# Gathering four expert rows of 32 tokens at a time, with weighted sums in four column quarters of TensorE

## The chip, the cores and the metric

The kernel runs on one core of one Trainium2 chip. The metric is the device time of one execution in microseconds, the lower the better; the median of several runs is compared. The traces come from one profiled execution of each kernel.

## What is computed

A decoder trunk of two layers over 256 tokens of width 1024, all in float32. Layer 0 mixes tokens with an S5 state-space layer (a complex diagonal scan over the positions, GELU, a gated projection); layer 1 with dilated sliding-window attention in three groups of 16 heads. Each layer ends in PEER, a channel mixer that fetches single-neuron experts. For each token and each of 8 heads it scores two halves of product keys, takes the best 16 of each, and of their sums the best 16: 128 experts for each token, with softmax gates. Then, for h the normalised token:

```python
def chunk_fn(args):
    hc, ic, gc = args
    act = jnp.einsum('cd,ckd->ck', hc, u_tab[ic])
    return jnp.einsum('ck,ckd->cd', gc * jax.nn.gelu(act), v_tab[ic])
```

The row of U and the row of V of an expert lie side by side, 2048 floats, 8 KB. A token fetches 128 of them, and the whole kernel 256 tokens x 128 x 2 layers: 537 MB of the 685 MB that it moves.

## The kernel before

The tokens are two chunks of 128, one token to a partition. There are four phases of gather: layer 0 with chunk 0 and 1, layer 1 with chunk 0 and 1. In each phase 128 gathers bring, each, one expert row for each of the 128 tokens (1.05 MB). They go two by two (a pair, 64 of them in a phase) through a ring of eight slots:

- POOL adds the two parts of the row numbers (L788), reads one of them back (L792) and issues two indirect DMAs (L794), after TensorE and VectorE are done with the pair four pairs back (L785, L786).
- VectorE takes the dot product of the U half of each slot with H (L826), ScalarE the gelu of two dots (L635), VectorE multiplies by the gates (L830).
- ScalarE builds a diagonal matrix of the weights (L639), and TensorE multiplies it with the V half of the slot, two matmuls of 512 columns that add up in PSUM banks 0 and 1 (L393). An f32 matmul shows as two weight loads and two MATMUL instructions in the trace.
- Where `both_on_pe` holds (the first 44, 8, 8 and 0 pairs of the four phases) both rows of a pair go to TensorE. Elsewhere the second is summed by VectorE (L838), and otherwise VectorE only sets a flag (L834).

The order on every engine is written out by hand. Class `Gather` has a method `at(phase, n)`, which puts the pairs up to n of a phase into an engine's stream; the rest of the work stands between such calls. So the second chunk's S5 (L929 to L972 on VectorE, L448 to L472 on TensorE, from pair 14 on, four pairs to each of eight steps) runs under phase 0. Layer 1 of chunk 0 runs under phase 1, of chunk 1 under phase 2: norm, three quarters of the top-k in twelve parts, 18 projections (L412) with a 2 MB weight load each, heads (L527 to L563, L1113), output projection, norm, key projections (L422). Phase 3 has only the top-k parts under it, three pairs apart, and the last norm of chunk 0. The top-k of a quarter of the heads is in four parts (L1015 to L1086); its row numbers are known when `idx_ready` rises (L1085), for which POOL waits once in a quarter (L801). Weights go by SyncE's queue into two buffers in turn (L343), each load when TensorE has used the buffer.

The norm (L852 to L862) squares on VectorE, takes the root on ScalarE (L645) and writes H, of which there is one for each chunk. At the end of a phase VectorE adds the banks to X (L850).

S5 on VectorE has eight tiles in two sets (M) for its products; the outputs come from matmuls with 32 columns of weights (L469), in an order that finishes one 32-partition strip of the bank before the next. Its inputs come from matmuls with 32 rows (L455).

```python
def pair(phase, b, r, first):
    ...
    if not first:
        pool.wait_ge(v_pe, b * SETS + (phase * PAIRS_G + r - SETS + 1))
        pool.wait_ge(v_dve, b * SETS + (phase * PAIRS_G + r - SETS + 1))
```

## Time and profile before

| | |
|---|---|
| runs | 1946.47, 1946.58, 1944.43 us; median 1946.47 |
| profiled execution | 1946.0 us, span 1944.2 |
| busy PE, DVE, ACT, POOL | 1388.8 (71%), 1444.4 (74%), 421.5 (22%), 874.3 us (45%) |
| mean granted TensorE clock | 0.873 |
| DMA | 685.04 MB (read from HBM 683.01), mean 352 GB/s |
| queue of the gathers | 536.90 MB, 69.4% of the 16 engines' span |
| queue of the weights | 147.20 MB, 18.3% |
| chain that ended last | PE 32%, DVE 30%, DMA 25%, issue 5%, ACT 4%, POOL 3% |

PE is TensorE's matmuls, PEld its weight loads, DVE is VectorE, ACT is ScalarE, SP is SyncE. The span goes from the first to the last instruction; the execution's own time is 1.8 us longer. The time of the phases can be read from the dot products: their first ones start at 187.9, 634.3, 1126.9 and 1593.3 us, and the last at 1930.8. A clock of 1.00 is 2.4 GHz, 0.50 is 1.2 GHz; a figure between is the mean of a stretch with both.

### The profile page before, as it was taken

How to read it: one execution, taken by the hardware profiler on the slowest of the kernel's cores; microseconds unless marked ns; L12 is line 12 of the kernel's file. 1: busy time of each engine (PE TensorE's matmuls, PEld its weight loads, DVE VectorE, ACT ScalarE, POOL GpSimd, SP SyncE). 2: the span in 40 equal slices, each digit the busy share in tenths (PEclk: the TensorE clock that was granted, in tenths of full speed). 3: DMA queues.
4: the chain of work that ended last, by engine and by line, in shares of the span. 5: the costliest groups of instructions: out<-in, count | busy, mean ns of one | idle time of the engine just before them, and what ended most of it. 6: DMA issues, size and time to landing. Idle time of an engine off the chain costs nothing.

```text
span 1944.2 us, 16899 instructions
## 1 busy us (share of the span) xinstructions
PE 1388.8 (71%) x4848; PEld 713.1 (37%) x4848; DVE 1444.4 (74%) x3260; ACT 421.5 (22%) x911; POOL 874.3 (45%) x1031
## 2 busy tenths in 40 slices
PE   1676766777976698898777559979987765544554
PEld 1446223333454243543536124355454541111111
DVE  8944987777568887655657788776576699899776
ACT  4011211111121212402411121162163111111111
POOL 0002443344444334344343853355465557666763
PEclk9888888889988899799789779999999887787777
DMA  7017977888999899899699989999999999999997
GB/s 287 1 66 288 348 282 298 318 330 322 369 423 422 317 404 424 310 421 423 254 408 411 412 342 390 425 403 380 425 406 375 422 353 389 378 366 365 414 421 300
DMA packets 88638, 685.04 MB, mean 352 GB/s; under 512 B 12144, under 2 KB 12272, under 8 KB 14320
## 3 DMA queue, kind: packets, MB, share of 16 engines
q0 software_dynamic: 73728, 536.90, 69.4%
q1 hardware_dynamic: 14832, 147.20, 18.3%
q8 instruction: 37, 0.61, 0.1%
q14 instruction: 41, 0.34, 0.0%
HBM read 683.01 MB, written 1.05 MB: 352 GB/s over the span
## 4 chain that ended last, share of the span: by engine, by line
PE 32%; DVE 30%; DMA 25%; issue 5%; ACT 4%; POOL 3%; POOLq 0%; SPq 0%; DVEq 0%
DMA ringmem<-experts,rows_now 16%; PE ps L393 12%; DVE ringmem L826 10%; PE ps L412 10%; DMA wt<-w_qkv 6%; PE ps L422 4%; DVE X L838 2%; DVE area L954 2%; DMA wt<-w_o 2%; PE ps L469 2%; POOL ringmem L794 2%; PE ps L536 2%; ACT gelus L635 1%; PE ps L561 1%; ACT diag L639 1%
## 5 line engine op out<-in xcount | busy, mean ns | idle before, releaser
L393 PE MATMUL ps<-ringmem,diag 128*128 128x512 f32 x1264 | 743.7, 729 | 416.5 <-ACT diag L639 416.0
L826 DVE CUSTOM_DVE_ANT_0 ringmem<-ringmem,H 128x1024 f32<-128x1024 f32 x512 | 610.8, 1220 | 86.0 <-DMA ringmem<-experts,rows_now 83.8
L794 POOL DMA_INDIRECT ringmem<-experts,rows_now x512 | 602.1, 1176 | 130.6 <-issue 118.3
L393 PEld LDWEIGHTS ps<-ringmem,diag 128*128 128x128 f32 x1264 | 265.0, 226 | 819.8 <-ACT diag L639 563.9
L788 POOL TENSOR_TENSOR rows_now<-row_a,row_b 128x2 uint32 (+1 forms) x256 | 130.5, 510 | 895.2 <-PE ps L393 708.3
L635 ACT ACTIVATE gelus<-dots 128x2 f32<-128x2 f32 x256 | 52.2, 204 | 993.6 <-DVE dots L826 993.3
L412 PE MATMUL ps<-wt,hT 128*128 128x512 f32 x576 | 254.5, 595 | 15.1 <-DMA wt<-w_qkv 15.1
L838 DVE SCALAR_TENSOR_TENSOR X<-ringmem,wts,X 128x1024 f32<-128x1024 f32 x196 | 251.9, 1285 | 7.5 <-DVE wts L830 0.5
L412 PEld LDWEIGHTS ps<-wt,hT 128*128 128x128 f32 x576 | 107.9, 190 | 158.1 <-issue 154.5
L792 POOL TENSOR_TENSOR tick<-rows_now 128x1 uint32<-128x1 uint32 x256 | 137.0, 535 | 20.2 <-POOL rows_now L788 0.3
L639 ACT ACTIVATE diag<-con,wts 128x128 f32<-128x128 f32 x316 | 120.3, 398 | 61.3 <-DVE wts L830 61.3
L830 DVE TENSOR_TENSOR wts<-gelus,gate 128x2 f32<-128x2 f32 x256 | 41.2, 161 | 111.6 <-ACT gelus L635 111.6
L422 PE MATMUL ps<-hT,wt 128*128 128x128 f32 x1024 | 119.9, 279 | 5.0 <-DMA wt<-w_q 3.8
L422 PEld LDWEIGHTS ps<-hT,wt 128*128 128x128 f32 x1024 | 118.8, 195 | 12.3 <-DMA wt<-w_q 6.3
L1104 DVE TENSOR_TENSOR area<-ps,con 128x512 f32<-128x512 f32 x24 | 16.6, 692 | 74.4 <-PE ps L412 74.3
L469 PE MATMUL ps<-area 128*32 128x128 f32 x512 | 51.0, 333 | 29.2 <-DVE area L972 29.2
L412 PE MATMUL ps<-wt,gT 128*128 128x512 f32 x128 | 62.0, 642 | 9.8 <-DMA wt<-w_o 8.4
L635 ACT ACT_TABLE_LOAD x50 | 64.2, 1283 | 0.9
L469 PEld LDWEIGHTS ps<-area 128*32 128x32 f32 x512 | 42.8, 134 | 37.0 <-DVE area L972 31.5
L1119 DVE CUSTOM_DVE_ANT_0 area<-ps,area 128x384 f32<-128x384 f32 (+1 forms) x32 | 24.2, 755 | 43.1 <-PE ps L536 43.1
L1019 DVE MAX8 qs<-ps 128x8 f32<-128x128 f32 x64 | 14.2, 283 | 43.8 <-PE ps L443 43.8
L954 DVE TENSOR_TENSOR_SCAN area<-area 128x128 f32<-128x128 f32 x128 | 45.8, 431 | 0.1
(155 smaller groups left out, 1132.4 us busy)
## 6 DMA issues: line engine op xcount, KB each, us to landing
wt<-w_qkv SPq DMA_DIRECT2D x36, 2048.0 KB, 11.5
wt<-w_q SPq DMA_DIRECT2D x16, 2048.0 KB, 11.8
wt<-w_glu SPq DMA_DIRECT2D x5, 2048.0 KB, 8.1
ringmem<-experts,rows_now POOLq DMA_INDIRECT x512, 10.1
wt<-w_o SPq DMA_DIRECT2D x4, 2048.0 KB, 14.8
ringmem<-w_glu SPq DMA_DIRECT2D x3, 2048.0 KB, 16.9
gain<-gains SPq DMA_DIRECT2D x9, 512.0 KB, 9.2
area<-keys SPq DMA_DIRECT2D x4, 1024.0 KB, 9.8
```

What stands on the lines that cost most here:

```text
L393: last = pe.matmul(ps[:, n, :], diag[:, r, i, :], ring[:, 2 * r + i, D + n * 512:D + (n + 1) * 512], start=(first and i == 0), stop=final, ...
L412: last = pe.matmul(ps[:, bank, :], act[:, k, :], wt[:, n % 2, k, :], start=(k == 0), stop=(k == KT - 1))
L422: last = pe.matmul(ps[:, bank, m * P:(m + 1) * P], wt[:, n % 2, k, m * P:(m + 1) * P], hT[:, k, :], start=(k == 0 and m == 0), stop=(k == ...
L469: last = pe.matmul(ps[32 * q:32 * (q + 1), 2, 0:P], CW[:, PPT * k + q, w, :], m[:, q, :], start=(i == 0), stop=(i == 3))
L635: act.activation(gelus[:, 2 * r:2 * r + 2], dots[:, 2 * r:2 * r + 2], ACT.Gelu_apprx_tanh).then_inc(gelu_ready, 1)
L639: last = act.activation(diag[:, r, i, :], ident, ACT.Copy, scale=wts[:, 2 * r + i:2 * r + i + 1])
L788: pool.tensor_tensor(rows_now[:, r, :], row_a[:, c, at], row_b[:, c, at], ALU.add).then_inc(rows_ready, 1)
L792: pool.tensor_tensor(tick[:, :], rows_now[:, r, 0:1], rows_now[:, r, 0:1], ALU.add)
L794: pool.indirect_dma_start(ring[:, 2 * r + i, :], None, experts[phase // NC], bass.IndirectOffsetOnAxis(ap=rows_now[:, r, i:i + 1], axis=0) ...
L826: last = v.tensor_tensor_reduce(ring[:, i, 0:D], ring[:, i, 0:D], H[:, c, :], 1.0, 0.0, ALU.mult, ALU.add, dots[:, i:i + 1])
L838: v.scalar_tensor_tensor(out=X[:, c, :], in0=ring[:, 2 * r + 1, D:2 * D], scalar=wts[:, 2 * r + 1:2 * r + 2], in1=X[:, c, :], op0=ALU.mult ...
L954: last = v.tensor_tensor_scan(dst[:, q, :], mag[:, n:n + 1].to_broadcast([P, P]), src[:, q, :], z0[:, n:n + 1] if c else 0.0, ALU.mult, AL ...
```

## The change

A gather now takes four expert rows of each of 32 tokens. Four gathers (a quad, 32 of them in a phase) serve all 128 tokens, and the bytes are the same. In slot j of a quad the partitions hold tokens 32j to 32j+31 four times over, each time with another expert. What follows from it:

- H is needed in four spread copies: Hrep[:, j] holds the 32 rows of quarter j four times. TensorE makes them with a matrix of repeated identities (`spread_h`), eight matmuls of 32 rows and 512 columns in each phase, and ScalarE copies each out of PSUM, at the start of a phase. There is one H instead of two, and the norm that writes it next waits for these matmuls.
- The weights are a matrix S[:, b, j] of 128 x 32 for each slot: the small identity times gate times gelu, two VectorE products for a quad. The diagonals on ScalarE, the flags and VectorE's own sums are gone.
- TensorE multiplies S[:, b, j], 32 columns, with the V half of the slot into partitions 32j to 32j+31 of banks 0 and 1: eight matmuls in a quad, the four j in turn for each half.
- The gelu is taken of four dots at once, and a slot is free again when its whole quad has gone through TensorE.
- The top-k gives floats of row number and gate for a quarter (`sel`). ScalarE lays them out anew with 16 copies of 32 partitions, and makes the row numbers integers with one more, before `idx_ready` rises. POOL's adds and reads are gone, and its instructions and all loops are written out.
- S5 has seven tiles instead of eight, with more ordered steps; its weights have two parts instead of three, with the sign put into a product; its matmuls are ordered so that the strips alternate. Keys, projected queries and head tiles share a smaller area, with the waits that this needs; the counts of PSUM use in attention are split in two semaphores.

```diff
-        H = sb("H", [P, NC, D])
+        H = sb("H", [P, D])
+        Hrep = sb("Hrep", [P, QUAD, D])
...
             def at(self, phase, n):
...
+                end = STEPS * phase + 2 * min(n, PAIRS_G)
+                while self.done < end:
+                    self.slot(self.done)
                     self.done += 1
...
         def _(pe):
+            def slot(s):
+                q, j = divmod(s, QUAD)
+                if j < QUAD - 1:
+                    return
+                phase, n = divmod(q, QUADS)
+                pe.wait_ge(s_ready, q + 1)
+                if n == 0 and phase:
                     pe.wait_ge(peer_done, phase)
...
+                for half in range(2):
+                    for j in range(QUAD):
+                        last = pe.matmul(ps[TG * j:TG * (j + 1), half, :], S[:, q % 2, j, :],
+                                         ring[:, (QUAD * q + j) % RING,
+                                              D + half * 512:D + (half + 1) * 512],
+                                         start=(n == 0), stop=(n == QUADS - 1), skip_group_check=True)
                 last.then_inc(v_pe, 1)
...
+            def spread_h(phase):
+                pe.wait_ge(normed, norm_event(phase // NC, phase % NC, 1) + 1)
+                for j in range(QUAD):
+                    rows_j = slice(TG * j, TG * (j + 1))
+                    for half in range(2):
+                        n = 2 * QUAD * phase + 2 * j + half
+                        if j:
+                            pe.wait_ge(hrep_ready, n - 1)
+                        pe.matmul(ps[:, 2 + half, :], rep[rows_j, :], H[rows_j, half * 512:(half + 1) * 512],
+                                  start=True, stop=True, skip_group_check=True).then_inc(h_spread, 1)
...
             layer0(None, 0)
+            spread_h(0)
             layer0(0, 1)
             g.at(0, PAIRS_G)
+            spread_h(1)
             layer1(1, 0)
             g.at(1, PAIRS_G)
+            spread_h(2)
             layer1(2, 1)
             g.at(2, PAIRS_G)
+            spread_h(3)
...
         def _(act):
+            def spread_h(phase):
+                if phase:
+                    act.wait_ge(dots_ready, QUADS * phase)
+                for j in range(QUAD):
+                    for half in range(2):
+                        act.wait_ge(h_spread, 2 * QUAD * phase + 2 * j + half + 1)
+                        act.copy(Hrep[:, j, half * 512:(half + 1) * 512],
+                                 ps[:, 2 + half, :]).then_inc(hrep_ready, 1)
...
             def gate_quarter(ph, i):
                 act.wait_ge(best_ready, QUARTERS * ph + i + 1)
+                act.activation(gex, gex, ACT.Exp).then_inc(gate_exp, 1)
+                n = QPQ * i
+                act.wait_ge(sel_ready, QUARTERS * ph + i + 1)
+                for j in range(QUAD):
+                    for r in range(QUAD):
+                        last = act.copy(lay[TG * r:TG * (r + 1), ph % NC, :, j, n:n + QPQ],
+                                        sel[TG * j:TG * (j + 1), :, QPQ * r:QPQ * (r + 1)])
+                link(last)
+                act.copy(rows[:, ph % NC, :, n:n + QPQ],
+                         lay[:, ph % NC, 0, :, n:n + QPQ]).then_inc(idx_ready, 1)
...
         def _(pool):
+            for s in range(2 * NC * STEPS):
+                phase, at = divmod(s, STEPS)
+                n, j = divmod(at, QUAD)
+                if at % QSTEPS == 0:
+                    pool.wait_ge(idx_ready, QUARTERS * phase + at // QSTEPS + 1)
+                if s >= RING:
+                    pool.wait_ge(v_pe, (s - RING) // QUAD + 1)
+                pool.indirect_dma_start(
+                    ring[:, s % RING, :], None, experts[phase // NC],
+                    bass.IndirectOffsetOnAxis(ap=rows[:, phase % NC, j, n:n + 1], axis=0)
+                ).then_inc(landed[s % RING], 16)
...
         def _(v):
+            def slot(s):
+                q, j = divmod(s, QUAD)
+                phase, n = divmod(q, QUADS)
+                c, b, i = phase % NC, q % 2, s % RING
+                if n == 0:
+                    v.wait_ge(hrep_ready, 2 * QUAD * phase + 2 * j + 2)
+                v.wait_ge(landed[i], 16 * (s // RING + 1))
+                last = v.tensor_tensor_reduce(ring[:, i, 0:D], ring[:, i, 0:D], Hrep[:, j, :],
+                                              1.0, 0.0, ALU.mult, ALU.add, dots[:, b, j:j + 1])
+                if j < QUAD - 1:
+                    return
                 last.then_inc(dots_ready, 1)
...
+                if q >= 2:
+                    v.wait_ge(v_pe, q - 1)
+                shape = [P, QUAD, TG]
+                link(v.tensor_tensor(S[:, b], spread(own, 1, shape), spread(lay[:, c, 1, :, n], 2, shape),
+                                     ALU.mult))
+                v.wait_ge(gelu_ready, q + 1)
+                v.tensor_tensor(S[:, b], S[:, b], spread(gelus[:, b, :], 2, shape),
+                                ALU.mult).then_inc(s_ready, 1)
...
-            def norm(gphase, start, c, e, done, count):
+            def norm(gphase, start, c, e, done, h_free, count):
...
+                if count:
+                    v.wait_ge(h_free, count)
+                v.scalar_tensor_tensor(out=H[:, :], in0=X[:, c, :], scalar=stat[:, 3:4],
...
             def s5_rotate(c, k):
...
+                v.tensor_tensor(T1, co, bre, ALU.mult)
+                v.tensor_tensor(T2, si, bim, ALU.mult)
+                link(v.tensor_tensor(T3, si, bre, ALU.mult))
+                link(v.tensor_tensor(T1, T1, T2, ALU.add))
+                v.tensor_tensor(T2, co, bim, ALU.mult).then_inc(bu_used, 1)
                 v.wait_ge(bu_used, u + 1)
+                link(v.tensor_tensor(T2, T2, T3, ALU.subtract))
```

## Rows read from the trace of the kernel before

**Rows 1.** Busy time by stretch: us, engines busy (instructions), PE clock, DMA share, GB/s.

```profile
180.00:274.00 94.00, 56.26 (x104) 22.54 (x104) 79.22 (x271) 21.44 (x47) 43.85 (x58) 0.82 0.89 340
274.00:487.00 213.00, 154.39 (x602) 72.90 (x602) 161.76 (x347) 30.88 (x103) 88.64 (x128) 0.87 0.83 311
487.00:634.00 147.00, 114.99 (x480) 66.24 (x478) 98.24 (x194) 24.76 (x55) 65.32 (x83) 0.88 0.98 405
634.00:1127.00 493.00, 388.97 (x1208) 199.82 (x1208) 339.39 (x764) 116.73 (x248) 220.84 (x255) 0.88 0.94 379
1127.00:1593.00 466.00, 390.39 (x1448) 214.55 (x1448) 342.90 (x757) 140.85 (x259) 233.25 (x253) 0.94 0.96 391
1593.00:1804.00 211.00, 102.66 (x152) 33.63 (x152) 192.62 (x432) 31.37 (x85) 138.49 (x153) 0.78 0.95 375
1804.00:1931.00 127.00, 71.42 (x100) 22.04 (x100) 97.21 (x153) 17.89 (x53) 77.26 (x93) 0.78 1.00 415
...
778.00:826.00 48.00, 38.64 (x142) 24.66 (x143) 29.49 (x61) 22.37 (x44) 16.90 (x25) 0.79 0.80 309
826.00:923.00 97.00, 86.84 (x219) 38.30 (x218) 54.88 (x96) 16.61 (x38) 42.03 (x45) 0.96 1.01 422
923.00:972.00 49.00, 38.45 (x143) 25.29 (x142) 29.85 (x61) 20.99 (x41) 16.48 (x26) 0.74 0.69 255
```

**Rows 2.** The chain of waits under S5 of the second chunk: start, us, what.

```profile
277.65 10.01 PE ps L393 x16
```

**Rows 3.** Groups by line: operation, count, busy us, mean ns, idle before them, its releaser.

```profile
L393 PE MATMUL ps<-ringmem,diag 128*128 128x512 f32 x1264 | 743.7, 729 | 416.5 <-ACT diag L639 416.0
...
L838 DVE SCALAR_TENSOR_TENSOR X<-ringmem,wts,X 128x1024 f32<-128x1024 f32 x196 | 251.9, 1285 | 7.5 <-DVE wts L830 0.5
...
L830 DVE TENSOR_TENSOR wts<-gelus,gate 128x2 f32<-128x2 f32 x256 | 41.2, 161 | 111.6 <-ACT gelus L635 111.6
```

**Rows 4.** Groups by line, small VectorE and ScalarE operations.

```profile
L739 ACT COPY area<-ps 128x512 f32<-128x512 f32 x24 | 14.1, 589 | 55.0 <-PE ps L523 55.0
...
L1110 DVE TENSOR_TENSOR area<-area 128x256 f32<-128x256 f32 x24 | 10.2, 425 | 0.8
...
L670 ACT ACTIVATE gate<-gate 128x32 f32<-128x32 f32 x16 | 3.7, 230 | 0.2
```

**Rows 5.** The timeline of two pairs in the last stretch: start, us, engine, operation.

```profile
1820.19 1.22 DVE L826 CUSTOM_DVE_ANT_0 ringmem<-ringmem,H 128x1024 f32<-128x1024 f32 x1
...
1821.45 0.20 ACT L635 ACTIVATE gelus<-dots 128x2 f32<-128x2 f32 x1 [4.60 <-DVE dots L826]
...
1822.34 3.27 PE L393 MATMUL ps<-ringmem,diag 128*128 128x512 f32 x4 [3.45 <-ACT diag L639]
...
1825.80 1.02 POOL L788 TENSOR_TENSOR rows_now<-row_a,row_b 128x2 uint32 x1 [1.82 <-PE ps L393]
...
1827.24 0.97 POOL L794 DMA_INDIRECT ringmem<-experts,rows_now  x1 [0.15 <-issue]
...
1827.69 1.98 PE L393 MATMUL ps<-ringmem,diag 128*128 128x512 f32 x4 [2.09 <-ACT diag L639]
...
1828.51 1.96 POOL L794 DMA_INDIRECT ringmem<-experts,rows_now  x1 [0.30 <-issue]
```

**Rows 6.** Busy time of L469 alone, 66 to 68 us: PE, PEld, clock, DMA.

```profile
66.00:68.00 2.00, 2.00 (x20) 1.70 (x20) 0.50 0.00 0
```

**Rows 7.** The timeline of TensorE at 72 us.

```profile
71.89 0.75 PE L455 MATMUL ps<-hT,area 32*128 32x128 f32 x16
```

**Rows 8.** Line 794 alone, from issue to landing.

```profile
DMA to landing us min/median/max: 5.3/10.1/27.6
```

**Rows 9.** The timeline at the end of the first phase.

```profile
627.46 1.23 DVE L826 CUSTOM_DVE_ANT_0 ringmem<-ringmem,H 128x1024 f32<-128x1024 f32 x1 [0.61 <-DMA ringmem<-experts,rows_now]
...
637.80 1.28 ACT L647 ACT_TABLE_LOAD   x1
...
639.53 1.29 DVE L861 SCALAR_TENSOR_TENSOR H<-X,stat,gain 128x1024 f32<-128x1024 f32 x1
```

More of the change, by code:

```diff
@@ L268, in build, with __init__ @@
         class Gather:
-            def __init__(self, eng, pair):
-                self.eng, self.pair, self.done = eng, pair, 0
+            def __init__(self, slot):
+                self.slot, self.done = slot, 0
             def at(self, phase, n):
@@ L451, in s5_bu @@
                     pe.wait_ge(bu_used, u)
-                for q in range(PPT):
-                    rows = slice(32 * q, 32 * (q + 1))
-                    for r in range(2):
-                        last = pe.matmul(ps[:, 4 + q, r * P:(r + 1) * P], WB[rows, k, r, :],
-                                         hT[rows, k, :], start=True, stop=True, skip_group_check=True)
+                for r in range(2):
+                    for q in range(PPT):
+                        quad = slice(32 * q, 32 * (q + 1))
+                        last = pe.matmul(ps[:, 4 + q, r * P:(r + 1) * P], WB[quad, k, r, :],
+                                         hT[quad, k, :], start=True, stop=True, skip_group_check=True)
                 last.then_inc(bu_ready, 1)
@@ L819, in link @@
                 v.wait_ge(dve, steps[0])
-            def pair(r, b, phase, bp, first, final, both):
-                c = phase % NC
-                for i in (2 * r, 2 * r + 1):
-                    v.wait_ge(landed[i], b * 16 + 16)
-                    last = v.tensor_tensor_reduce(ring[:, i, 0:D], ring[:, i, 0:D], H[:, c, :],
-                                                  1.0, 0.0, ALU.mult, ALU.add, dots[:, i:i + 1])
-                last.then_inc(dots_ready, 1)
-                v.wait_ge(gelu_ready, b * SETS + (r + 1))
-                v.tensor_tensor(wts[:, 2 * r:2 * r + 2], gelus[:, 2 * r:2 * r + 2],
-                                gate[:, c, bass.ds(bp * RING + 2 * r, 2)], ALU.mult).then_inc(wts_ready, 1)
-                v.wait_ge(wts_ready, b * SETS + (r + 1))
-                if both:
-                    v.tensor_copy(passed[:, :], wts[:, 2 * r:2 * r + 1]).then_inc(v_dve, 1)
-                    return
-                if not (first and phase == 0):
-                    v.wait_ge(v_dve, b * SETS + r)
-                v.scalar_tensor_tensor(out=X[:, c, :], in0=ring[:, 2 * r + 1, D:2 * D],
-                                       scalar=wts[:, 2 * r + 1:2 * r + 2], in1=X[:, c, :],
-                                       op0=ALU.mult, op1=ALU.add).then_inc(v_dve, 1)
@@ L844, in peer_end @@
+            g = Gather(slot)
             def peer_end(phase):
```

282 lines of the change are left out of this document (115 added, 167 removed).

## The prediction

> **What bounds the kernel now.** I read first the busy time by stretch, cut where the dot products change their pace. The DMA share is near 1, and the rate 422 GB/s, in the stretch from 826 to 923 us [rows 1]: that is the fastest rate held for long. Against it each stretch has room of its length times (1 - rate/422): 18 us in 180 to 274, 56 in 274 to 487, 6 to 634, 49 to 1127, 34 to 1593, 24 to 1804, 2 to 1931 [rows 1]: 189 us. The bytes don't change, so no schedule of them gains more: 1946 - 189 = 1757 us is the floor. The two stretches of attention heads of the first chunk, 778 to 826 and 923 to 972, ran at 309 and 255 GB/s [rows 1]: 13 + 19 of the 49.
>
> Who holds back the DMA differs. In 274 to 487 (S5 of the second chunk over the first gather) the chain of waits goes through 10 us of weighted-sum matmuls, one after another, ahead of the next S5 input [rows 2], while VectorE is busy 162 of 213 us [rows 1]. In 1593 to 1804 (the last gather over the top-k) VectorE is busy 193 of 211 [rows 1]. In 1804 to 1931 the DMA binds, at 415 GB/s. Groups by line give the sizes: 744 us of TensorE in L393, 252 of VectorE in the sums at L838 [rows 3].
>
> **What goes and comes.** Per four rows (a quad): out go two weight products, eight diagonal builds at most, 16 matmul instructions of full width (or half of them, with two sums on VectorE at 1.285 us [rows 3]), and two adds and two ticks on POOL. In come two VectorE products of 128x128 and 16 matmul instructions of 32 columns. VectorE's products: 128x256 takes 0.425 [rows 4], 128x2 0.161 [rows 3]; between them I take 0.3 each, and keep both as bounds (256 of them at the upper end would be 33 us more over the run, half of it under the DMA).
>
> TensorE, the disputed price. A pair of these instructions (one f32 matmul of 512 columns) takes about 0.86 us at full clock, 2.4 GHz (1.98 for four with the tail), and 1.7 at the half, 1.2 GHz (3.27 for four, partly at each) [rows 5]. Do four column quarters run at once? In the S5 outputs, also 32 columns wide, 20 instructions of 128 columns started in 2.00 us at a granted clock of 0.50 [rows 6]; one such instruction alone lasts about 0.21 us at that clock (a quarter of 0.85), so two quarters ran at once, there in an order that serves one quarter eight times in a row. Row strips in the S5 inputs did 16 in 0.75 us [rows 7], where one by one at full clock is 1.7: all four at once. The change alternates quarters, as these. So a quad costs from 2 x 0.86 + 0.2 = 1.9 us (four at once, full clock) to 8 x 1.7 = 13.7 (none at once, half clock). I take four at once, 1.9 full, 3.7 half, as rows 7 is nearest in order. The Trainium skill (TensorE: Matmul & The Clock Gate, Part 3) gives 3.07 times for four row strips and 2.38 for three column strips, not the ideal; by it a quad is 13.7/3.07 = 4.5 us at half clock, and the sum below would be some 20 us worse, in the last gather mostly; no row here shows four column strips.
>
> **The ring.** It was freed by pairs, four of them; now by quads, two. Gathers at the full rate land 2.47 us apart (1.05 MB at 422 GB/s). The shortest issue to landing is 5.3 us [rows 8]. A slot's successor must land five spacings, 12.3 us, after the quad's last landing, so its issue may come 7.0 us after it. The chain: dot and gelu 1.46 (1820.19 to 1821.65), product 0.4, matmuls 3.7, POOL 0.2 (1825.61 to 1825.80), with half a microsecond of waits [rows 5]: 6.2. That fits by 0.8 us, by 2.6 at full clock. POOL loses the 1.4 us of add and tick (1825.80 to 1827.24); but its issue lasted 1.96 instead of 0.97 when a dot ran beside it [rows 5], which can eat the rest. Before, the same slot had three more pairs, 14.8 us, as cover.
>
> **The sum**, against the profiled execution (1946.0 us, span 1944.2; median of the runs 1946.47).
> - S5 under the gather, 8 steps of 26.6 us (POOL's 128 instructions, four a pair, make 32 pairs). VectorE is busy 20.2 per step [rows 1]; it loses 4 x 0.16 (weights) and as many flags, gains 4 x 0.3, has some 0.3 for three more ordered waits, and waits some 2 us in all for gelus: 22.5. TensorE's 10 us become under 4, off the path; S5's products wait for the outputs before them, done a step earlier. (22.5 - 26.6) x 8 = -33.
> - Top-k ahead of it, 180 to 274, and at the first quads of the second gather: VectorE-bound (79 of 94 us busy [rows 1]), no L838 there, so the same work: -3 with the rest up to 634.
> - Heads, first chunk: 11 pairs, TensorE's share of a pair falls from 3.4 to 1.85 at half clock, and ScalarE switches its table for gelu half as often: -1.7 each, -18. Second chunk: -9, within its room there. Projection stretches are at the DMA's rate already; other transitions -5. TensorE's projections have less company; each is 16 instructions of 0.43, 6.9 us at full clock; at 0.85, between the 0.96 and 0.74 of rows 1, it is 8, and its 2.1 MB with its pair's take the DMA 9.9: covered by 1.9.
> - Last gather, 1593 to 1804: 153 POOL instructions make 38 pairs of 5.55 us [rows 1]. Of that 2.4 are dots, 0.46 weights with their wait, 1.285 the sum, so 1.4 the third of a top-k part (4.2 us). Now 2.4 + 0.5 + 1.4 = 4.3, under the 4.93 of the DMA. Parts that fall inside a quad delay its end by some 1.5 us, of which 0.8 is covered, nine times with the rest: I recover 13 of the 24 us.
> - New, the four copies of H at each phase: eight matmuls and eight ScalarE copies of 0.589 us [rows 4], alternating over two banks, behind the last quad's matmuls and ahead of the square root of the next norm on ScalarE. From the last dot's start: quad done 5.7, matmuls to 15, copies to 15.8, table switch (1.28 [rows 9]) and root to 17.3, norm done 18.9; now it is done 13.4 after (627.46 to 640.82) [rows 9]. +5.5 at two boundaries; at the third the DMA runs dry: the fourth copy at 16.4, quad freed 22.5, data 25.3, against 19.7 when the other quad has landed: +5.6. Together +17. Below zero is excluded, as the copies wait for the last dots; above, 14 us of matmuls at half clock make it 30.
> - New, 17 small ScalarE copies per quarter, 0.230 us for the nearest row [rows 4], 4 us: later quarters lie 2 or more pairs ahead of need and are covered by those pairs' transfers; without that cover each costs 4. ScalarE waits there for VectorE's selection, with the next quad's gelu queued behind; VectorE does no dot meanwhile, so that gelu isn't asked for. The first is on the path, and the second chunk's norm now waits for the copies of H: +5.
> - POOL's other adds and ticks: nothing, since POOL waited for TensorE; it is the ring's 1.4 us, counted. SyncE's order and bytes stay. The loops written out: nothing, as most steps were written out before and no row shows a wait for instructions; if POOL's 512 issues did wait for them, it would be B.
> Sum: -33 - 3 - 27 - 5 - 13 + 17 + 5 = -59: **1887 us**, on the profiled time.
>
> **Rivals.**
> A. Nearly all the room is used: jitter hides in VectorE's freed time, boundaries hide behind landed quads. Two thirds of 189: 1820 us. For: 59 + 22 of cost is only 81. Against: VectorE-bound stretches keep their work. 0.12.
> B. Slower, the shallow ring. Place: every quad where gathers alone feed the DMA. Point: last landing to next issue over 7.0 us. At 9 (half clock, POOL held by a dot, a ScalarE or TensorE block in between) the 32 quads of the last gather lose 2 each, 64, the 13 go, and ten quads elsewhere lose 20: 1887 + 97 = 1984. For: 6.2 against 7.0, and TensorE gets less to do, with the granted clock already 0.78 in both last stretches [rows 1]. Against: S5 stretches leave 22.5 per 19.8. 0.14.
> C. The quarters don't run at once, so the change doesn't do what it says. Then a quad takes 6.9 us at full clock, the chain 9.3, the last gather loses 32 x 2.3 = 74, and S5 and heads gain nothing: 1946 + 74 + 22 - 13 = 2029. Against: rows 6. 0.05.
> D. The boundaries and inner pauses give the gains back, by the 30 us bound and double losses in quads: 1930 to 1950. 0.09.
> Another floor: were the DMA held to its mean of 352 GB/s, nothing would be gained; rows 1 hold 422 over 97 us. The Trainium skill (DMA: Bandwidth & Descriptors, Bandwidth) speaks of about 358 GB/s per core with both cores of a pair streaming, and of 425 for one alone; by the first, 683 MB take 1908 us and D would be likeliest; the trace goes with the second.
>
> **Numbers.** The forecast has 0.60 (own range 1850 to 1930, from the bounds of the quad price, the boundaries and heads). About 0.2% (4 us) is what can be told from no change. Faster: 0.60 + 0.12 + 0.04 of D = 0.76; same 0.05; slower 0.14 + 0.05 = 0.19. 1845 to 1975 leaves out two thirds of A, C and half of B: 0.2.
>
> **What would show it.** Four weighted-sum matmuls with starts a few ns apart, a quad in 1.9 or 3.7 us; VectorE near 1444 - 252 - 50 + 77 = 1219 us; S5 steps of 22.5 us; the rate in 1593 to 1804's counterpart over 395 GB/s; dots idle about 9 us at each phase start. Wrong, if the pure gather at the end runs under 400 GB/s (B), or quads take 7 us or more (C).

## The result, and the profile after

The changed kernel takes **1978.15 us** (median of four runs, 1969.89 to 1980.83), against 1946.35 for the kernel before on the same chip (1944.43 to 1946.58): a ratio of 1.0158, interval 1.0126 to 1.0191. It is 32 us slower, where 1887 and "faster" were forecast; 1978 lies 3 us above the range of 1845 to 1975. The profiled execution has a span of 1979.0 us and a mean granted TensorE clock of 0.729, where it was 0.873. It is the slowest of the four runs, so tables that are read from it can be some microseconds too long beside a median.

The page of the changed kernel: busy time and share by engine, clock in tenths over 40 slices, DMA, the chain that ended last, and the groups that the change brings (operation, count, busy us, mean ns, idle time ahead of them and its releaser).

```profile
PE 1131.4 (57%) x5696; PEld 545.9 (28%) x5696; DVE 1220.7 (62%) x2986; ACT 319.6 (16%) x748; POOL 542.8 (27%) x519
PEclk9878556667785897896886579879867876555555
DMA packets 88642, 685.21 MB, mean 346 GB/s; under 512 B 12144, under 2 KB 12272, under 8 KB 14320
DMA 34%; PE 32%; DVE 20%; POOL 6%; issue 5%; ACT 2%; SPq 0%; POOLq 0%; DVEq 0%; ACTq 0%
...
L816 POOL DMA_INDIRECT ringmem<-experts,lay x512 | 539.0, 1053 | 1412.2 <-PE ps L380 1115.0
L839 DVE CUSTOM_DVE_ANT_0 ringmem<-ringmem,Hrep 128x1024 f32<-128x1024 f32 x512 | 617.0, 1224 | 367.8 <-DMA ringmem<-experts,lay 357.3
L380 PE MATMUL ps<-ringmem,S 128*32 128x512 f32 x2048 | 390.9, 904 | 653.1 <-DVE S L852 653.1
L852 DVE TENSOR_TENSOR S<-S,gelus 128x128 f32<-128x128 f32 x128 | 37.5, 293 | 48.1 <-ACT gelus L644 34.3
L690 ACT COPY lay<-sel 32x16 f32<-32x16 f32 x256 | 51.5, 201 | 66.8 <-DVE sel L1096 64.0
L397 PE MATMUL ps<-H,con 32*128 32x512 f32 x64 | 45.6, 1017 | 3.3 <-ACT Hrep L656 3.3
```

All engines have less to do, as intended: TensorE 1131 us instead of 1389, VectorE 1221 (the forecast said 1219) instead of 1444, POOL 543 instead of 874. Yet the run is longer. Two lines point to where to look. POOL now stands idle for 1115 us until a weighted-sum matmul (L380) frees ring slots; before, it waited 708 us for L393. And the clock row (PEclk) ends in six fives, half clock, 1.2 GHz. Neither shows by itself that time is lost.

Busy time by stretch, the counterparts of [rows 1] (from and to, us, then PE, PEld, DVE, ACT and POOL busy with instructions, PE clock, DMA share, GB/s). First top-k, S5, the rest of the first gather, the second and third gathers, the last gather over the top-k, the pure gather at the end; below, gathers 320 to 347, with projections and then the second half of the second chunk's heads.

```profile
187.00:275.00 88.00, 28.30 (x111) 6.63 (x110) 78.15 (x258) 21.33 (x56) 24.45 (x27) 0.53 0.86 328
275.00:460.00 185.00, 56.48 (x592) 19.94 (x592) 161.56 (x312) 10.18 (x41) 68.37 (x63) 0.66 0.89 355
460.00:614.00 154.00, 103.23 (x574) 56.04 (x575) 77.44 (x179) 19.16 (x44) 44.91 (x43) 0.78 0.98 404
614.00:1119.00 505.00, 344.59 (x1448) 170.60 (x1448) 273.40 (x690) 89.15 (x211) 131.27 (x128) 0.76 0.91 369
1119.00:1625.00 506.00, 375.05 (x1691) 201.49 (x1690) 278.59 (x693) 107.16 (x218) 141.12 (x131) 0.80 0.90 362
1625.00:1835.00 210.00, 74.07 (x315) 13.37 (x313) 151.23 (x394) 26.11 (x85) 79.00 (x77) 0.58 0.96 383
1835.00:1966.00 131.00, 43.36 (x192) 7.14 (x192) 66.61 (x123) 5.23 (x15) 46.11 (x45) 0.55 0.96 387
...
1379.00:1490.00 111.00, 86.39 (x380) 51.30 (x380) 49.45 (x103) 26.82 (x41) 31.28 (x28) 0.76 0.89 357
```

And the same gathers (320 to 347 of 512) in the kernel before:

```profile
1377.00:1470.00 93.00, 81.21 (x327) 46.73 (x325) 65.07 (x117) 41.55 (x69) 54.67 (x55) 0.96 0.99 403
```

S5 gained what it should (213 us at 311 GB/s became 185 at 355). The third gather, at 391 GB/s before, fell to 362; the clock of gathers 320 to 347 from 0.96 to 0.76. The last stretch fell from 415 GB/s to 387 though DMA is all it has to do; under 400 was the forecast's own sign for rival B.

A table in stages that don't depend on where a window is cut: microseconds between the first dot products of the named gathers (gather 0 to 511; a phase has 128). Q, K and V are the projections ahead of the heads, WO is the one behind them.

```
stage, gathers           before   after  change
to the first dot          187.9   195.4   +7.5
0-24 (top-k)               86.2    79.6   -6.6
24-88 (S5)                211.3   185.2  -26.1
88-128                    148.9   153.7   +4.8
128-184 (QKV, heads)      234.0   241.1   +7.1
184-256 (QKV, heads, WO)  258.7   264.5   +5.8
256-296 (QKV)             157.2   161.0   +3.8
296-320 (heads, QKV)       92.5    98.8   +6.3
320-348 (QKV, heads)       93.1   110.8  +17.7
348-384 (heads, WO)       123.6   134.8  +11.2
384-456 (top-k)           199.7   192.6   -7.1
456 to the end            151.2   161.7  +10.5
```

The heads themselves fill shorter stretches, two in each chunk (us, with the granted clock):

```
gathers          before        after
163-174          45.0 (0.77)   46.5 (0.59)
196-208          48.6 (0.72)   41.7 (0.63)
292-312          64.4 (0.98)   73.0 (0.77)
336-353          48.9 (1.00)   62.6 (0.72)
```

The first chunk's heads gained 5 us and the second chunk's lost 22. Most of the rest that gathers 128 to 384 lost lies in the stretches between them, where the DMA ran at 393 to 418 GB/s before.

The chain of waits through the heads of the second chunk, after and then before (start, us, what):

```profile
1448.75 1.51 PE ps L546 x6
1450.27 2.45 PE ps L560 x12
1452.72 2.87 PE ps L535 x12
...
1458.66 0.85 PE ps L546 x6
```

```profile
1438.01 0.85 PE ps L547 x6
1438.86 1.29 PE ps L561 x12
1440.14 1.55 PE ps L536 x12
```

The same 30 instructions of one head last 6.83 us instead of 3.69, all on the chain, with a granted clock of 0.50 where it was 1.00. It is not so for every head: the next one, from 1458.66 on, is back at full clock. Of the last five blocks of 30, three take 6.8 us and two 3.7; before, all take 3.7. So the theory is that relief of TensorE took away its clock, and that the heads paid. The Trainium skill (TensorE: Matmul & The Clock Gate, Part 1) says the throttled clock is the default and activity releases it; the trace agrees, with 0.96 at 81 of 93 us busy before and 0.76 at 86 of 111 after in gathers 320 to 347.

The ring, in the timeline of the last stretch (start, us, engine, line, operation):

```profile
1869.71 1.23 DVE L839 CUSTOM_DVE_ANT_0 ringmem<-ringmem,Hrep 128x1024 f32<-128x1024 f32 x1 [1.24 <-DMA ringmem<-experts,lay]
...
1875.05 1.23 DVE L839 CUSTOM_DVE_ANT_0 ringmem<-ringmem,Hrep 128x1024 f32<-128x1024 f32 x1 [1.65 <-DMA ringmem<-experts,lay]
1876.08 1.00 POOL L816 DMA_INDIRECT ringmem<-experts,lay  x1 [5.55 <-PE ps L380]
...
1879.97 1.23 DVE L839 CUSTOM_DVE_ANT_0 ringmem<-ringmem,Hrep 128x1024 f32<-128x1024 f32 x1 [1.23 <-DMA ringmem<-experts,lay]
1881.12 0.29 DVE L849 TENSOR_TENSOR S<-con,lay 128x128 f32<-128x128 f32 x1
1881.24 0.20 ACT L644 ACTIVATE gelus<-dots 128x4 f32<-128x4 f32 x1 [10.06 <-DVE dots L839]
1881.55 0.29 DVE L852 TENSOR_TENSOR S<-S,gelus 128x128 f32<-128x128 f32 x1
1881.89 3.64 PE L380 MATMUL ps<-ringmem,S 128*32 128x512 f32 x16 [6.62 <-DVE S L852]
1883.99 1.23 DVE L839 CUSTOM_DVE_ANT_0 ringmem<-ringmem,Hrep 128x1024 f32<-128x1024 f32 x1 [2.15 <-DMA ringmem<-experts,lay]
...
1885.84 0.94 POOL L816 DMA_INDIRECT ringmem<-experts,lay  x1 [5.03 <-PE ps L380]
```

The quad's own chain is as forecast: dot, gelu, two products of 0.29, a quad of 3.64 us at half clock. But the data issued at 1876.08 arrive at 1883.99, and the dot before was at 1879.97: a gap of 4.0 us where landings at the full rate are 2.47 apart. Of the last 14 quads six begin 3.5 to 6.2 us after the dot ahead of them, the others 2.2 to 2.5. The six are 10.4 us over 2.47 in sum, which is the whole loss of 456 to the end. From issue to landing, in 1874 to 1880, in the pure gather 1835 to 1960, and in the last gather of the kernel before, 1804 to 1926:

```profile
DMA to landing us min/median/max: 7.9/9.7/11.6
...
DMA to landing us min/median/max: 7.6/10.3/13.9
...
DMA to landing us min/median/max: 10.3/11.8/13.8
```

The ring was sized with the run's shortest, 5.3 [rows 8]. Two cautions. The profile holds no landing for one slot of the ring, 64 of the 512 gathers; one of these has its dot 6.5 us after its issue, so 7.6 is not the shortest. And the time to land includes the gathers ahead in the queue: the four of the quad issued from 1876.08 on land 7.9, 9.1, 10.4 and 11.6 us after their issues, and the time is longest, 10.3 us at least, where the queue never runs short.

### The profile page after: what moved, and what is told of

Same layout as the page of the kernel before. It is cut to its first block, busy times and chain, and to the rows that moved or that the text cites. A ratio compares the mean times of both kernels' runs of the same rounds, so it can differ in the third digit from the quotient of the medians.

```text
span 1979.0 us, 16308 instructions
## 1 busy us (share of the span) xinstructions
PE 1131.4 (57%) x5696; PEld 545.9 (28%) x5696; DVE 1220.7 (62%) x2986; ACT 319.6 (16%) x748; POOL 542.8 (27%) x519
## 4 chain that ended last, share of the span: by engine, by line
DMA 34%; PE 32%; DVE 20%; POOL 6%; issue 5%; ACT 2%; SPq 0%; POOLq 0%; DVEq 0%; ACTq 0%
DMA ringmem<-experts,lay 25%; PE ps L380 10%; PE ps L412 10%; DMA wt<-w_qkv 7%; POOL ringmem L816 6%; DVE ringmem L839 6%; PE ps L422 4%; PE ps L535 2%; DVE area L965 2%; PE ps L397 2%; PE ps L560 2%; PE ps L546 1%; DVE S L852 1%; DMA wt<-w_o 1%; DVE area L1132 1%
## 5 line engine op out<-in xcount | busy, mean ns | idle before, releaser
L816 POOL DMA_INDIRECT ringmem<-experts,lay x512 | 539.0, 1053 | 1412.2 <-PE ps L380 1115.0
L839 DVE CUSTOM_DVE_ANT_0 ringmem<-ringmem,Hrep 128x1024 f32<-128x1024 f32 x512 | 617.0, 1224 | 367.8 <-DMA ringmem<-experts,lay 357.3
L380 PE MATMUL ps<-ringmem,S 128*32 128x512 f32 x2048 | 390.9, 904 | 653.1 <-DVE S L852 653.1
L380 PEld LDWEIGHTS ps<-ringmem,S 128*32 128x32 f32 x2048 | 69.0, 143 | 906.7 <-DVE S L852 754.8
L690 ACT COPY lay<-sel 32x16 f32<-32x16 f32 x256 | 51.5, 201 | 66.8 <-DVE sel L1096 64.0
L535 PE MATMUL ps<-area 64*128 64x128 f32 x288 | 55.0, 358 | 1.8 <-DVE mx L1132 1.8
L535 PEld LDWEIGHTS ps<-area 64*128 64x128 f32 x288 | 47.6, 255 | 11.9 <-issue 7.6
L560 PEld LDWEIGHTS ps<-area 128*128 128x128 f32 x288 | 48.5, 256 | 2.6 <-issue 2.5
L560 PE MATMUL ps<-area 128*128 128x64 f32 x288 | 48.9, 333 | 0.0
L965 DVE TENSOR_TENSOR_SCAN area<-zs,area 128x128 f32<-128x128 f32 x128 | 47.6, 435 | 0.6
## 6 DMA issues: line engine op xcount, KB each, us to landing
ringmem<-experts,lay POOLq DMA_INDIRECT x512, 10.5
```

Of the source, the lines that this page charges most:

```text
L380: last = pe.matmul(ps[TG * j:TG * (j + 1), half, :], S[:, q % 2, j, :], ring[:, (QUAD * q + j) % RING, D + half * 512:D + (half + 1) * 512 ...
L535: last = pe.matmul(ps[:, 2 + at // 512, at % 512:at % 512 + P], QT[rows, gr, h // 2, :], kt, start=True, stop=True, skip_group_check=True)
L560: last = pe.matmul(ps[:, 7, h * DH:(h + 1) * DH], PT[u % 2][:, j * P:(j + 1) * P], vv, start=(j == 0), stop=(j == n - 1), skip_group_check ...
L690: last = act.copy(lay[TG * r:TG * (r + 1), ph % NC, :, j, n:n + QPQ], sel[TG * j:TG * (j + 1), :, QPQ * r:QPQ * (r + 1)])
L816: pool.indirect_dma_start(ring[:, s % RING, :], None, experts[phase // NC], bass.IndirectOffsetOnAxis(ap=rows[:, phase % NC, j, n:n + 1], ...
L839: last = v.tensor_tensor_reduce(ring[:, i, 0:D], ring[:, i, 0:D], Hrep[:, j, :], 1.0, 0.0, ALU.mult, ALU.add, dots[:, b, j:j + 1])
```

## The experiments

The theory: (clock) less matmul work lowers the granted clock, and stages that hang on a chain of matmuls get longer; (ring) freeing eight slots in fours starves the gather queue. The rivals: it is one alone; or the new copies of H and small ScalarE copies; or the quads themselves. The medians of the kernel before, run beside each group below, are 1946.0 to 1948.0 us, so medians from different groups can be compared to about 2 us.

**Half the sums taken from the kernel before.** This asks whether relief of TensorE helps at all. The weighted sums of columns 512 to 1023 are left out, but for the first and last of a phase.

```diff
-                    for n in range(2):
+                    for n in range(2 if first or final else 1):
                         last = pe.matmul(ps[:, n, :] ...
```

> The kernel before, with the weighted sums of output columns 512 to 1023 left out except in the first and last pair of a phase: half of TensorE's weighted-sum matmuls are gone (about 370 us of busy time), nothing is added, and ring and loads stay. Clock theory: the time barely falls or even rises (1935 to 1960), as the granted clock falls below 0.8 and the heads of the second chunk of layer 1 take longer than the 79 and 48 us they took. Theory that TensorE's work is what costs: it falls by 25 us or more, to 1920 or less.

Measured: 1948.1 us against 1948.0, ratio 0.9999 (0.9979 to 1.002), clock 0.728 instead of 0.873, inside what the clock theory allowed. Gathers 320 to 347:

```profile
1363.00:1475.00 112.00, 97.49 (x297) 61.82 (x296) 65.16 (x115) 41.38 (x68) 52.30 (x54) 0.67 0.85 344
```

S5 fell from 211.3 to 184.0 us, as in the changed kernel, and the stages 296 to 348 rose from 185.6 to 223.0 with the clock at 0.67. Nothing else had changed: 139 us less of TensorE's busy time were worth 27 us in one place and cost 37 in another. All ten blocks of 30 instructions in the second chunk's heads now take 6.8 us where each took 3.7. This shows the clock mechanism by itself, with neither quads nor copies of H nor a coarser ring.

**The ring of the kernel before, freed by four rows.**

```diff
-                    pool.wait_ge(v_pe, b * SETS + (phase * PAIRS_G + r - SETS + 1))
-                    pool.wait_ge(v_dve, b * SETS + (phase * PAIRS_G + r - SETS + 1))
+                    more = 1 - r % 2
+                    pool.wait_ge(v_pe, b * SETS + (phase * PAIRS_G + r - SETS + 1 + more))
+                    pool.wait_ge(v_dve, b * SETS + (phase * PAIRS_G + r - SETS + 1 + more))
```

> The kernel before, with one edit: the first pair of every two waits for one more pair before its gathers are issued, so the ring is released by four rows as in the changed kernel, with all other work unchanged. Ring theory: this alone costs a large part of what was missing, 25 to 60 us (1971 to 2006). Clock theory: the granted clock stays at 0.87, so the release of four costs little, 0 to 12 us (1946 to 1958), most of it in the last phase.

Measured: 2019.1 us, ratio 1.0356 (1.0329 to 1.0383): **+71 us** for a wait alone, at a clock of 0.853, and more than the 1971 to 2006 that the ring theory gave. It is not only in the pure gather at the end, which lost 8.5 of it (402 to 389 GB/s, the last rows of before and of this kernel):

```profile
1793.00:1931.00 138.00, 76.66 (x111) 23.60 (x110) 105.94 (x168) 19.10 (x57) 86.69 (x104) 0.79 0.97 402
```

```profile
1858.00:2006.00 148.00, 83.48 (x111) 26.26 (x111) 106.63 (x167) 19.10 (x57) 86.17 (x104) 0.71 0.97 389
```

The gather over the top-k (384 to 456) lost 18.7, gathers 184 to 256 lost 12.2, gathers 88 to 128, 128 to 184 and 348 to 384 some 8 each, and S5 only 0.9.

**Zero matmuls in the last phase of the changed kernel**, four behind each quad but the last: they add nothing to the sums and only keep TensorE busy.

```diff
                 last.then_inc(v_pe, 1)
+                if phase == 3 and n < QUADS - 1:
+                    fill(4)
```

with `fill` a loop of `pe.matmul(ps[:, i % 2, :], zero[:, :], con[:, 0:512], start=False, stop=False)`.

> The changed kernel, and in the last phase four more full-width matmuls of zero weights behind every quad but the last, after the quad's slots are released. Clock theory (the weighted sums lost 0.8 us a quad because TensorE has less to do and its granted clock is 0.55 there): the clock of the stretch from 1835 to 1966 us rises to 0.8 or more, a quad's matmuls fall from 3.64 to about 1.9 us, release comes 1.7 us earlier, and the stretch goes from 387 GB/s to 410 or more; the time falls by 5 to 15 us below the changed kernel's 1978. Ring theory (two quads are too few slots whatever the clock): the clock rises, but the rate stays under 395 GB/s and the time within 4 us of 1978, or it rises, as the added matmuls stand ahead of the next quad's.

Measured: 1966.5 us, ratio 1.0093 (1.0062 to 1.0124), 12 us less than the changed kernel. In the last 145 us:

```profile
1809.00:1954.00 145.00, 100.41 (x336) 30.49 (x328) 75.70 (x138) 5.43 (x16) 53.55 (x52) 0.82 0.98 397
```

The clock rose from 0.56 to 0.82, the rate from 386 to 397 GB/s, and 456 to the end fell from 161.7 to 156.5. That lies between the two theories' bounds (410 or more, under 395). So half clock is part of the ring's loss, but at 0.82 this end is still 5 us longer than before (151.2). The rest of the 12 us lies ahead of this end, most of it in phases where nothing was added, so it is no effect of the filling.

**Zero matmuls in the heads of the changed kernel**, two of full width a head ahead of the transposes, both chunks.

```diff
                         if 2 <= i < NH + 2:
+                            fill(2)
                             attn_pt(c, half, i - 2)
```

> The changed kernel, and in the attention heads of layer 1 two full-width matmuls of zero weights for each head, ahead of the transposes that wait for the softmax (64 more matmuls, 55 us of TensorE at the full clock). Clock theory: the clock there rises from 0.71 to 0.76 to above 0.85, and the heads of the second chunk, gathers 320 to 384 of the program in 111, 50 and 85 us, take 10 us less each or better, although TensorE has more to do: total 1950 to 1970. Theory that TensorE's work itself holds the heads: they take longer by what was added, 28 us or more in the second chunk, and the total is over 1990.

Measured: 1942.25 us, ratio 0.998 (0.9963 to 0.9996), **36 us less** than the changed kernel, by 64 matmuls of work that is thrown away, and less than the 1950 to 1970 expected. Gathers 184 to 207 (projections, then heads of the first chunk) in the changed kernel, then the same and gathers 320 to 347 with the filling:

```profile
855.00:950.00 95.00, 74.61 (x304) 40.73 (x304) 41.73 (x96) 21.07 (x42) 26.68 (x25) 0.75 0.84 339
```

```profile
842.00:929.00 87.00, 72.75 (x328) 36.11 (x328) 42.04 (x96) 21.05 (x42) 25.73 (x24) 0.96 0.92 376
...
1348.00:1448.00 100.00, 85.08 (x408) 46.08 (x408) 48.78 (x103) 26.89 (x42) 30.10 (x28) 0.90 0.94 383
```

More instructions (328 for 304), less busy time (72.75 us for 74.61), clock 0.96 for 0.75: the clock is the cause of the heads' loss, and not a sign of it. The four stretches of heads take 40.0 us (clock 0.93), 34.7 (1.00), 65.5 (0.97) and 54.6 (0.97), where the changed kernel had 46.5, 41.7, 73.0 and 62.6: 29 us less in the profiled executions, nearly half of them in the first chunk, where the kernel before ran at a low clock too. TensorE's busy time of the whole run stays at 1132 us.

**Zero matmuls in the kernel before**, in the first chunk's heads, which had a clock of 0.77 and 0.72 even there.

```diff
                         if 2 <= i < NH + 2:
+                            fill(2 if c == 0 else 0)
                             attn_pt(c, half, i - 2)
```

> The kernel before with the same 32 added matmuls in the first chunk's heads, where its granted clock is 0.81 and 0.76 (53 and 64 us). Clock theory: even there more work on TensorE costs nothing or gains, 1936 to 1947, with the clock of those two stretches above 0.9. If TensorE's work is what holds them, 32 matmuls of 0.86 us or more are added, 28 us: 1970 or above.

Measured: 1941.63 us, ratio 0.9978 (0.9964 to 0.9991). Gathers 184 to 207, before and with the filling:

```profile
868.00:965.00 97.00, 80.01 (x248) 43.65 (x248) 55.47 (x107) 31.91 (x64) 37.74 (x48) 0.84 0.85 343
```

```profile
867.00:961.00 94.00, 84.37 (x283) 43.74 (x284) 55.64 (x108) 32.00 (x64) 37.45 (x48) 0.95 0.89 353
```

The clock of the heads goes up to 0.93, and the median falls by 4.5 us. That is little, but the interval of the ratio lies below 1: the effect doesn't need the change.

**Copies of H in the first phase only**; the later dots use the old copies, so the values are those of another H, and the time is that without `spread_h(1)` to `spread_h(3)`.

```diff
-            spread_h(1)
...
-                if n == 0:
-                    v.wait_ge(hrep_ready, 2 * QUAD * phase + 2 * j + 2)
+                if q == 0:
+                    v.wait_ge(hrep_ready, 2 * j + 2)
```

> The changed kernel with the copies of H made in the first phase alone; the later phases take their dots with the first phase's copies, so those outputs are left to be something else. It prices the term of the prediction for the phase starts (17 us for three). If that term was right, 1978 falls by 12 to 22 us, and the time from a phase's last dot to the next one's first falls from 8 to 10 us to 3 to 6. If the starts cost more than seen, as behind a stalled ring, it falls by 30 or more.

Measured: 1954.19 us, ratio 1.0046 (1.003 to 1.0061): the copies cost 24 us, where the forecast had 17 (bounds 0 and 30), between the two outcomes expected (12 to 22, or 30 and more). From the last dot of a phase to the first of the next the three boundaries take 6.8, 7.3 and 5.4 us before, 9.9, 7.9 and 10.0 after, and 8.2, 8.1 and 7.2 here, not the 3 to 6 expected. Most of the 24 lies behind them, in the first gathers of the second and third phase, which come 7 us sooner (33.3 instead of 40.9 for gathers 128 to 138, and of 40.6 for 256 to 266). In the timeline of the first boundary of the changed kernel:

```profile
609.45 6.76 PE L397 MATMUL ps<-H,con 32*128 32x512 f32 x9
...
611.61 0.59 ACT L656 COPY Hrep<-ps 128x512 f32<-128x512 f32 x1 [6.18 <-PE ps L397]
...
613.88 1.23 DVE L839 CUSTOM_DVE_ANT_0 ringmem<-ringmem,Hrep 128x1024 f32<-128x1024 f32 x1 [1.62 <-ACT Hrep L656]
```

**The changed kernel, worked through in pairs**: gelus, products, matmuls and release for two rows at a time; layout, copies of H and column quarters are kept.

```diff
-                if j < QUAD - 1:
+                if j % 2 == 0:
                     return
...
-                pe.wait_ge(s_ready, q + 1)
+                pe.wait_ge(s_ready, s // 2 + 1)
...
-                    for j in range(QUAD):
+                    for j in two:
...
-                    pool.wait_ge(v_pe, (s - RING) // QUAD + 1)
+                    pool.wait_ge(v_pe, (s - RING) // 2 + 1)
```

> The changed kernel worked through by pairs: gelu, S and the column-quarter matmuls of two slots at a time, with the slots released by pairs as before. TensorE runs two quarters at a time, so it is busy about 1.9 times as long in the sums, its clock rises above 0.8, and the ring is fine again. Clock and ring theories both expect a gain over the changed kernel: 1978 to between 1925 and 1955, with the second chunk's heads (87 and 60 us) back under 82 and 52 us if the clock is the cause there. If neither is (the copies of H, the layout of the row numbers), it stays within 8 us of 1978.

Measured: **1903.14 us**, ratio 0.9759 (0.973 to 0.9788): 75 us below the changed kernel, 45 below before, and below the 1925 to 1955 expected. Two things changed at once here, the release and the clock (0.828 for 0.729, since two column quarters at a time keep TensorE busy longer, 1330 us for 1131). So the release alone was put back:

```diff
-                    pool.wait_ge(v_pe, (s - RING) // 2 + 1)
+                    pool.wait_ge(v_pe, 2 * ((s - RING) // QUAD + 1))
```

> The changed kernel worked through by pairs (1903 us), with one edit: POOL waits for the whole quad before it reuses its first slot. Work, order and TensorE's load stay as by pairs, only the ring is coarse. Ring theory, as the kernel before lost 71 us by the same edit: 1903 rises by 25 to 70 us, to 1928 to 1973. Clock theory alone: it rises by less than 12, and all of the gain by pairs came from the clock.

Measured: 1974.17 us, ratio 1.0147 (1.0114 to 1.018): **+71 us** over the pairs, 1 us above the ring theory's range, at the same clock (0.824). The last stretch, in pairs and with the coarse release:

```profile
1752.00:1890.00 138.00, 78.96 (x228) 12.98 (x224) 79.13 (x168) 8.35 (x31) 64.56 (x52) 0.74 0.98 405
```

```profile
1807.00:1952.00 145.00, 81.99 (x228) 13.47 (x224) 79.10 (x168) 8.42 (x31) 59.79 (x52) 0.74 0.98 396
```

And gathers 320 to 347 with the coarse release, to be set beside the 111 us of the changed kernel:

```profile
1383.00:1479.00 96.00, 81.39 (x384) 41.25 (x384) 51.12 (x118) 36.07 (x55) 31.69 (x28) 0.98 0.98 401
```

Here the two causes part. At the same clock the ring costs 71 us. And with the same coarse ring these gathers take 96 us at a clock of 0.98 and 111 at 0.76. Not all of the 15 us need be the clock's, as pairs stand against quads too; the quads with zero matmuls, on the same coarse ring, took 100 us at 0.90.

**Both kinds in one kernel**: quads where VectorE binds (the first 24 gathers of the first three phases), pairs and their release elsewhere.

```diff
+def by_quad(s):
+    return s < 3 * STEPS and s % STEPS < 24
...
-                    pool.wait_ge(v_pe, (s - RING) // QUAD + 1)
+                    pool.wait_ge(v_pe, DONE[s - RING])
```

`DONE[s]` counts the pairs and quads up to gather s.

> By quads in the first 24 gathers of the first three phases, where VectorE's top-k holds the time (there quads took 80, 41 and 41 us against 90, 44 and 44 by pairs, as they save VectorE a product and a wait), and by pairs elsewhere. If these stretches add up as they stand, 10 + 3.5 + 3.5 us come off 1903: 1880 to 1892. If the clock is carried from stretch to stretch, or the switch stalls the ring, it stays at 1898 or above.

Measured: 1893.34 us, ratio 0.973 (0.9695 to 0.9766), 10 us below the pairs. Gathers 0 to 24 take 79.5 us, as with quads, instead of 89.6, and S5 179.7. The total is 1 us above the range for stretches that add up. The same with the zero matmuls in the first chunk's heads:

> The mixed version (1893 us) with two full-width matmuls of zero weights for each head of the first chunk of layer 1, where its clock is lowest. If the clock still costs something there, those heads (gathers 184 to 208 and 228 to 256 of the program, 91 and 76 us) shorten by 3 to 8 us in all and the total is 1883 to 1891; if the added matmuls cost as much as the clock gives, it stays within 4 us of 1893.

Measured: 1889.29 us, ratio 0.9704 (0.9683 to 0.9724). The runs of the two overlap (1889.21 to 1897.92, 1884.55 to 1897.72), so the filling is worth nothing that can be told here. It did raise the clock of the first chunk's heads, from 0.70 and 0.67 to 0.92, but they fell by 0.9 and 1.8 us only, and the second chunk's heads were at 0.94 and 0.97 without it. Either beats both kernels, by 52 to 57 us against before.

## Why the prediction was wrong

**The direction and the mechanism**: wrong. The sum had 59 us of gain; the measurement is 32 of loss. Step by step:

- *Four quarters at once*, 1.9 or 3.7 us a quad: right. 3.64 us at half clock for 16 instructions which one by one would be 13.7 by the forecast's price, so an estimated 3.8 times. The Trainium skill (TensorE: Matmul & The Clock Gate, Part 3) has 2.38 for three column strips; these four did better. Rival C falls.
- *Products of 0.3 each*: right, 0.288 and 0.293.
- *S5*: -33 forecast, -26 measured, with 22.5 a step forecast and 185.2/8 = 23.2 measured. *Top-k and the rest to 634*: -3 forecast, -6.6 + 4.8 = -2 measured.
- *The copies of H*: +17 forecast, +24 by the run without them. *The head*: +5, measured +7.5. The copies' mechanism is right and its size too small (the head's was not tested); the boundaries were worked out up to the first dot, and the matmuls and the second half of the copies delay the dots behind it too.
- **"Heads, first chunk -18, second chunk -9, within its room"**: the first step that failed. It let the price of the quads follow the clock and left the head's other matmuls at the clock they had. Measured in the heads alone: first chunk -5, second chunk +22. There some heads take 6.3 to 6.8 us on the chain and others 3.7 to 4.3, where all took 3.7. The run with half the sums shows that the relief alone costs this; the filled run shows that the clock alone gives most of it back (15 of the 22 us, and another 13 in the first chunk; -36 us on the median of the whole). The same step's *projections 0, "covered by 1.9"* took a clock of 0.85 for granted. It was 0.90 in gathers 174 to 196 and 312 to 336, and still the stretches between the heads lost some 29 us; with the coarse release alone, in the kernel before, the same stretches lost 34. That part is the ring's.
- **The ring, "fits by 0.8"**: the second, and the larger. The chain was forecast at 6.2 us. From the last dot's start to the next issue it is 5.9 (1879.97 to 1885.84), or 6.4 where a dot ran beside the issue (1869.71 to 1876.08); that half was right. What failed is "the shortest issue to landing is 5.3" as the lead that a full gather stream needs: that is the shortest of the whole run, at the start of the last gather, with an earlier gather still on its way. Behind the chain of 6.4 us the next quad but one had its first dot 7.9 us after the issue, 14.3 us in all where the full rate has 12.3. The four quads that came late from 1880 us on took 7.6 to 8.2 from issue to dot. No single time would have sized the ring, as the time to land grows with what is ahead in the queue (10.3 us at least in the last gather before); the price of the coarse release is measured, +71 us, and not derived. The Trainium skill (DMA: Bandwidth & Descriptors, Latency and other measured facts) says that HBM's latency rises under high load, and that lighter load lowers a DMA's fixed cost; no run here tells that from waiting behind gathers ahead.
- *Last gather -13*: measured -7.1 in 384 to 456 and +10.5 behind it, +3 in all. VectorE was relieved as forecast (151 of 210 us busy where it was 193 of 211), and the DMA rose only from 375 to 383 GB/s, under the 395 that was to show it. The coarse release alone made these gathers 18.7 us longer in the kernel before.

Rival B's number, 1984, is near the result, and its chance was 0.14. Its price was a shallow ring, which is the larger half of the truth; its place was wrong. B put the loss in "every quad where gathers alone feed the DMA", mostly the last gather. The two coarse-release runs have it over all phases: of 74 us between the profiled executions of before and of its coarse ring, 27 lie in the last gather from 384 on and 47 ahead of it, beside heads and projections. Rival A (1820) would have needed a DMA at its full rate nearly everywhere. D's price, the boundaries, is real but some 24 us. A likely reason, argued and not shown: where one engine or another delays a quad by a few microseconds anyhow, four slots of lead don't ride over it.

How the parts add: 75 us lie between the changed kernel and its pairs; 71 of them are the release. The other 4 are what is left of two things that nearly cancel, with the coarse release in both kernels: by pairs the second chunk's heads take 22 us less at a clock of 1.00, and gathers 0 to 88 and 384 to 456 take 23 us more. A slow chain costs at the fine release too: with half the sums left out the second chunk's heads lost 33 us. So pairs mend both losses, and as far as these runs tell the two add roughly. How the 71 would split at a clock of 0.73 was not tried, nor quads of four quarters whose slots come free one pair at a time, nor a deeper ring. What is shown is that the forecast's gains exist: with the release by two rows and the clock held, the same design gives 1893, near the 1887 of the sum.

## What to carry to other kernels

- Before work is taken from TensorE, read the granted clock and the chain of waits in every stage that hangs on matmuls: if the removed work is what holds 2.4 GHz there, price those stages at 1.2 GHz (here 6.8 us for 3.7 a head, which some heads paid and, with half the sums gone, all). Half the weighted sums gone was worth 0 us.
- A change of batch size is a change of release granularity. Don't size a ring with the shortest issue-to-landing time of the run (5.3 us, too short), nor with that of the busy stretch (10.3 us at least, which contains the queue). Coarsen the wait in the kernel you have and run it: three changed lines would have shown the 71 us ahead of the change. Batching and releasing can be chosen apart, and by stage.

## What the runs showed of the hardware

- Discarded zero matmuls can shorten a kernel: 64 of them took 36 us from the changed one and lowered TensorE's busy time in gathers 184 to 207 from 74.6 us to 72.8, with the clock going from 0.75 to 0.96.
- Four column quarters with 32 columns each overlap nearly fully also with f32 data in two instructions a product: an estimated 3.8 times (13.7 over 3.64 us), at half clock.
- POOL's issue of an indirect gather takes 0.94 us, also where a dot of VectorE starts after it; one that begins while a dot runs ends some 0.8 us after the dot. The timeline of the first boundary shows both: the issue at 603.83 against the dot at 603.96, and the one at 614.42 against the dot of 613.88 to 615.11.

```profile
603.83 0.94 POOL L816 DMA_INDIRECT ringmem<-experts,lay  x1 [0.30 <-issue]
603.96 1.23 DVE L839 CUSTOM_DVE_ANT_0 ringmem<-ringmem,Hrep 128x1024 f32<-128x1024 f32 x1 [1.23 <-DMA ringmem<-experts,lay]
...
614.42 1.50 POOL L816 DMA_INDIRECT ringmem<-experts,lay  x1 [0.30 <-issue]
```

- Freeing eight slots in fours instead of pairs cost 71 us in two kernels with quite different work per row: the granularity counts by itself. In the kernel before the rate of the run fell with it from 352 to 339 GB/s.
